# First projections in two-term pieces, setup loads in halves, and four more places for expert weights

## The reference

```python
def first_block(...):                       # x 512x1024, ctx 256x1024
    sh1, sc1, g1, sh2, sc2, g2 = adaln_params(c, w_mod)      # silu(c) @ w_mod + b_mod, six parts of 1024
    hx = modulate(rms_norm(x, norm1_g), sh1, sc1)            # h * (1 + scale) + shift
    hc = modulate(rms_norm(ctx, norm1_g), csh1, csc1)
    y_x = token_mix(hx, hc, w_in, ...)      # projections; gated scan in two directions, 4 heads;
                                            # attention, 8 heads over 2 KV heads, keys of ctx and x; gated merge
    x = x + g1 * y_x
    x = x + g2 * expert_choice_moe(modulate(rms_norm(x, norm2_g), sh2, sc2), w_router, w_gate, w_up, w_down)
    return rms_norm(x, final_norm_g)
def expert_choice_moe(h, ...):              # 16 experts, each takes its best 64 of 512 tokens
    gate, idx = top_k(softmax(h @ w_router).T, 64)
    hid = silu(h[idx] @ w_gate) * (h[idx] @ w_up)            # 1024 -> 1024, per expert
    return zeros.at[idx].add((hid @ w_down) * gate)
# second_block: projections, sparse attention, short convolution, and a feed-forward of 4096 features
```

## Time and profile before

| | us |
|---|---|
| median of 3 runs (1909.41 to 1919.11) | 1913.41 |
| the profiled execution's own time | 1913.68 |
| its span, first to last instruction | 1912.4 |
| PE busy | 1721.0 (90%) |
| DVE busy | 796.1 (42%) |
| ACT busy | 570.9 (30%) |
| mean granted TensorE clock | 0.965 of 2.4 GHz |
| bytes moved | 329.4 MB, mean 172 GB/s |

### The profile page before, as it was taken

One profiled execution on the slowest core, in us unless ns is written; L12 is line 12 of the kernel. 1 busy time (PEld: TensorE's weight loads), 2 busy tenths in 40 slices (PEclk: granted clock), 3 DMA queues, 4 the chain that ended last, 5 costly groups with the idle time before them and its releaser, 6 DMA issues.

```text
span 1912.4 us, 20334 instructions
## 1 busy us (share of the span) xinstructions
PE 1721.0 (90%) x8150; PEld 1123.7 (59%) x8150; DVE 796.1 (42%) x1325; ACT 570.9 (30%) x1026; POOL 117.2 (6%) x123
## 2 busy tenths in 40 slices
PE   5989899886999996998888888999888899999999
PEld 2656667564877773333332333687544678888877
DVE  2164655456633432021120211547577434444444
ACT  2224563564343321110110100431544442222221
POOL 0002121012100001000000000000100001010010
PEclk9999899988999997999999999999999899999999
DMA  8221201123323267999999999443400122222301
GB/s 311 89 74 44 89 23 45 67 89 132 102 75 133 95 267 277 424 424 424 422 424 424 425 423 419 152 131 88 132 1 1 45 88 88 88 88 93 111 18 45
DMA packets 93185, 329.40 MB, mean 172 GB/s; under 512 B 7828, under 2 KB 22820, under 8 KB 68516
## 3 DMA queue, kind: packets, MB, share of 16 engines
q1 hardware_dynamic: 86032, 315.80, 42.6%
q10 hardware_dynamic: 5716, 8.05, 1.3%
q0 software_dynamic: 1344, 4.25, 0.6%
HBM read 322.83 MB, written 4.20 MB: 171 GB/s over the span
## 4 chain that ended last, share of the span: by engine, by line
PE 66%; DMA 16%; DVE 9%; ACT 6%; issue 2%; ACTq 0%; SPq 0%; DVEq 0%
PE PS L672 21%; PE PS L1061 9%; PE PS L815 8%; DMA room<-in_w_exp_up_dram 8%; PE PS L413 7%; DMA ring<-in_w_exp_gate_dram 6%; PE PS L409 3%; PE PS L544 3%; PE PS L626 3%; PE PS L888 2%; PE PS L469 1%; DMA ring<-in_w_in_dram 1%; PE PS L698 1%; PE PS L826 1%; PE PS L1003 1%
## 5 line engine op out<-in xcount | busy, mean ns | idle before, releaser
L1791 DVE TENSOR_TENSOR wR<-ring,wR 128x1024 fp32r<-128x1024 f32 (+2 forms) x134 | 151.4, 1130 | 223.3 <-ACT wR L1176 223.2
L1176 ACT CAST wR<-ring 128x1024 fp32r<-128x1024 f32 (+2 forms) x134 | 130.0, 971 | 203.5 <-PE PS L1061 126.5
L1061 PE MATMUL PS<-wR,hR 128*128 128x512 f32 x768 | 176.2, 390 | 8.9 <-DVE tmp L2571 6.9
L672 PE MATMUL PS<-xR,wR 128*128 128x512 f32 x768 | 175.6, 389 | 0.9 <-DVE wR L1791 0.9
L1061 PEld LDWEIGHTS PS<-wR,hR 128*128 128x128 f32 x768 | 143.5, 188 | 41.5 <-DVE tmp L2571 9.6
L672 PEld LDWEIGHTS PS<-xR,wR 128*128 128x128 f32 x768 | 144.0, 188 | 31.1 <-issue 1.3
L815 PE MATMUL PS<-room,xeT 128*64 128x512 f32 x512 | 115.7, 595 | 27.2 <-DMA room<-in_w_exp_up_dram 15.1
L672 PE MATMUL PS<-hR,wR 128*128 128x512 f32 x528 | 128.5, 405 | 8.2 <-DVE wR L1791 5.6
L815 PE MATMUL PS<-ring,xeT 128*64 128x512 f32 x512 | 117.4, 604 | 19.3 <-DMA ring<-in_w_exp_up_dram 15.8
L672 PEld LDWEIGHTS PS<-hR,wR 128*128 128x128 f32 x528 | 103.2, 197 | 34.3 <-issue 8.7
L672 PE MATMUL PS<-hR1h,wR 128*128 128x512 f32 x320 | 102.2, 394 | 2.4 <-DVE wR L1791 2.4
(11 more groups left out here) (469 smaller groups left out, 2628.7 us busy)
## 6 DMA issues: line engine op xcount, KB each, us to landing
ring<-in_w_exp_gate_dram SPq DMA_DIRECT2D x32, 1024.0 KB, 27.6
room<-in_w_exp_gate_dram SPq DMA_DIRECT2D x32, 1024.0 KB, 28.1
ring<-in_w_exp_up_dram SPq DMA_DIRECT2D x32, 1024.0 KB, 26.4
room<-in_w_exp_up_dram SPq DMA_DIRECT2D x32, 1024.0 KB, 27.4
ring<-in_w_exp_down_dram SPq DMA_DIRECT2D x32, 1024.0 KB, 26.5
room<-in_w_exp_down_dram SPq DMA_DIRECT2D x32, 1024.0 KB, 27.8
ring<-in_w_mod_dram SPq DMA_DIRECT2D x12, 2048.0 KB, 7.9
ring<-in_w_in_dram SPq DMA_DIRECT2D x11, 2048.0 KB, 9.3
```

Of the source, the lines that this page charges most:

```text
L672: mm = T.matmul(b, o[s][:, k, :], x(t, k), start=(k == ks[0] and j == 0), stop=(k == ks[-1] and j == 2))
L1061: mm = T.matmul(down[m], uR[:, r % 2, s, k, 128 * i:128 * i + 128], o[t][:, 0, 512 * q:512 * q + 512], start=(k + j == 0), stop=(k == 3 an ...
L1176: A.copy(parts(wR, chunks, n)[0], W.view(unit)[:, ks, cs]).then_inc(act_hi.sem, act_hi.up(key))
L1791: V.tensor_tensor(lo, W.view(unit)[:, ks, cs], hi.bitcast(F32), ALU.subtract) \
```

## The change

- The first projections (`aq`, `akv`, and `f`, `q`, `v` of heads 0 and 1) become three-term products. Their weights are cut into twelve chunks (`first_chunks`), each rounded and subtracted into one of a few buffers `wS`; the tokens are stored in two pieces too (`hS`).
- The loads of the setup change order and size: `mod 0`, `mod 2` (shift and scale of features 0 to 511), the first half of `aq` (its first four k), then `mod 1`, `mod 3`, the context, the second half of `aq`. PE, ACT and DVE follow that order: `aq` runs k pair by k pair over four open banks.
- A unit of 256 columns takes one slot instead of two; slots are released by `sub_lo` instead of by PE.
- Ten small loads move from ACT's queue to POOL's, behind DVE's `low(7)`.
- `head_norm` of the queries comes before that of the keys.
- Router: logarithm and exponential instead of root and reciprocal, with the table loaded ahead; the first search round reads PSUM; the store of `h2k` in four parts; products wait for two k of `xeT` at a time.
- Experts: a ninth permanent extra place (`strips`) and three that are used once; the pieces 18, 7 and 15 are requested last of the first twenty, 18 only when `h2k` has been stored.

```diff
+MOD_ORDER = (0, 2, 1, 3)
...
+    FIRST = (0, 6, 2, 0, 4, 3)
+    ONCE = {7: "gathered", 15: "gathered", 19: "mixed"}
...
+            if k == 2 and n in self.ONCE:
+                slots = [NS + len(more) + list(self.ONCE).index(n)]
+                n += 1
+            elif k == 2:
+                if not cycle:
+                    cycle = [(at + j) % NS for j in range(NS)]
+                    cycle[4:4] = range(NS, NS + 4)
+                    cycle += range(NS + 4, NS + len(more))
+                slots = [cycle[turn % len(cycle)]]
+                turn, n = turn + 1, n + 1
             else:
-                size, top = 1 if k * n <= 2048 and k <= 4 else 2, 4 if 4 <= i < whole else NS
-                at = 0 if at + size > top or i == whole else at
+                if cycle:
+                    at, cycle = (at + turn % (NS + len(more))) % NS, []
+                size, top = 1 if k * width <= 2048 else 2, 4 if i < whole else NS
+                at = self.FIRST[i] if i < 6 else 0 if at + size > top or i in (6, whole) else at
...
+    def order(self):
+        first = self.number["gate", 0, 0, 0]
+        late = (18, 7, 15)
+        ahead = [n for n in range(20) if n not in late]
+        return [*range(first), *(first + n for n in (*ahead, *late)), *range(first + 20, len(self.units))]
...
-    u = [(("mod", j), *cols(d["w_mod"], 512 * j, 512)) for j in range(4)]
-    u += [("aq", *cols(d["w_in"], 2560, 512)), ("akv", *cols(d["w_in"], 3072, 256))]
+    first = [(("mod", j), *cols(d["w_mod"], 512 * j, 512)) for j in range(4)]
+    aq = [(("aq", x), *cols(d["w_in"][512 * x:512 * x + 512], 2560, 512)) for x in range(2)]
+    u = [first[0], first[2], aq[0], first[1], first[3], aq[1]]
+    u.append(("akv", *cols(d["w_in"], 3072, 256)))
...
+    once = [Area(nc, at, at + 2048).take(name, [128, 2048]) for name, at in
+            (("once7", DYN + 15456), ("once15", DYN + 13408), ("once19", DYN + 3072))]
...
+    first_chunks = [(("aq", k), ("aq", k // 4), slice(k % 4, k % 4 + 2), slice(0, 512), k % 4 == 2) for k in range(0, 8, 2)]
+    first_chunks += [(("akv", c), "akv", slice(4 * c, 4 * c + 4), slice(0, 256), c == 1) for c in range(2)]
+    first_chunks += [((x + "0", h), (x, 0), slice(0, 8), slice(128 * h, 128 * h + 128), h == 1) for x in "fq" for h in range(2)]
+    first_chunks += [(("v0", c), ("v", 0), slice(4 * c, 4 * c + 4), slice(0, 256), c == 1) for c in range(2)]
...
+        if chunks is first_chunks:
+            return [t.rearrange("p (a b) -> p a b", b=b) for t in ((wS1a, wS[3]) if n == 1 else wS[2 * (n % 2):2 * (n % 2) + 2])]
...
+            for k in range(4):
+                turn_x(early, k)
+            mod_turn(mods, 0)
+            mod_product(mods, 2)
+            turn_x(early, 4)
...
+        def token_terms(b, w, i, ks, start, stop):
+            for n, k in enumerate(ks):
+                for j, (s, t) in enumerate(TERMS):
+                    mm = T.matmul(b, hS(s, k, 128 * i, 128 * i + 128), w[t][:, n, :], start=(start and n + j == 0),
+                                  stop=(stop and n == len(ks) - 1 and j == 2))
+            return mm
...
+            def chunk(n, tiles):
+                w = parts(wS, first_chunks, n)
+                for i in tiles:
+                    if i == 0:
+                        T.wait_ge(*dve_lo["aq", 2 * n])
+                        for k in range(2 * n, 2 * n + 2):
+                            T.wait_ge(*dve_in["lx", k])
+                    if n == 0:
+                        bs.append(four.take(T, ("aq", i), act_in["aq", i]))
+                    mm = token_terms(bs[i], w, i + 2, range(2 * n, 2 * n + 2), n == 0, n == 3)
...
+            chunk(0, range(4))
+            mod_product(mods, 1)
+            mod_product(mods, 3)
+            chunk(1, range(2))
+            mod_turn(mods, 1)
+            mod_turn(mods, 3)
+            chunk(1, range(2, 4))
...
+            chunk(2, range(4))
...
+            chunk(3, range(4))
+            pool = Banks(0, 8)
+            bs = []
+            for c in range(2):
+                T.wait_ge(*dve_lo["akv", c])
+                w = parts(wS, first_chunks, 4 + c)
+                if c == 0:
+                    T.wait_ge(*dve_in["lc", 7])
+                for i in range(6):
+                    if c == 0:
+                        bs.append(pool.take(T, ("akv", i), act_in["av", i]))
+                    mm = token_terms(bs[i][:, 0:256], w, i, range(4 * c, 4 * c + 4), c == 0, c == 1)
...
+            for h in range(2):
+                b = pool.take(T, ("f", 0, h), act_scan["f", 0, h], 2)
+                T.wait_ge(*dve_lo["f0", h])
+                w = parts(wS, first_chunks, 6 + h)
+                feature_terms(b[:, 0:512], w, 256, 768)
+                feature_terms(b[:, 512:768], w, 0, 256).then_inc(pe_scan.sem, pe_scan.up(("f", 0, h)))
...
+        W.free["gathered"] = s_ga, 16
         router()
+        W.free["strips"] = pe_moe["aff"]
...
+            squares(range(2, 6), s_x)
+            root(2, 6)
+            A.wait_ge(*dve_in["A1", 0])
+            tokens(1)
+            copy_hi(wS, first_chunks, 0)
+            tokens(3)
+            copy_hi(wS, first_chunks, 1)
+            squares(range(2), s_x2)
+            copy_hi(wS, first_chunks, 2)
+            A.wait_ge(*dve_in["A1", 1])
+            tokens(5)
+            tokens(7)
+            root(0, 2)
+            copy_hi(wS, first_chunks, 3)
             for k in range(8):
                 A.wait_ge(*pe_in["hc", k | 1])
-                o = 256 * (k % 2)
-                A.activation(hT[:, k, 0:256], bank(("hc", k & 6))[:, o:o + 256], ACT.Identity, bias=modc[:, k, 1:2],
-                             scale=A1[:, 1, k:k + 1]).then_inc(s.sem, s.up(("hc", k)))
+                b = bank(("hc", k & 6))[:, 256 * (k % 2):256 * (k % 2) + 256]
+                for to, key in ((hT[:, k, 0:256], "hc"), (hSc[:, k, :], "hic")):
+                    A.activation(to, b, ACT.Identity, bias=modc[:, k, 1:2], scale=A1[:, 1, k:k + 1]) \
+                        .then_inc(s.sem, s.up((key, k)))
...
+            copy_hi(wS, first_chunks, 4)
             for i in range(4):
                 A.wait_ge(*pe_in["aq", i])
                 A.copy(aq[:, i, :], bank(("aq", i))).then_inc(s.sem, s.up(("aq", i)))
+            copy_hi(wS, first_chunks, 5)
+            root("q", 32)
+            copy_hi(wS, first_chunks, 6)
             for i in range(6):
                 A.wait_ge(*pe_in["akv", i])
                 A.copy(akv[:, i, :], bank(("akv", i))[:, 0:128]).then_inc(s.sem, s.up(("ak", i)))
                 A.copy(avs[:, i, :], bank(("akv", i))[:, 128:256]).then_inc(s.sem, s.up(("av", i)))
-            A.wait_ge(*dve_in["lb"])
-            A.activation(lbt[:, 1:3, :], lbt[:, 1:3, :], ACT.Exp).then_inc(s.sem, s.up("lb"))
-            for name in ("k", "q"):
-                A.wait_ge(*dve_in["ms", name])
-                n = {"k": 12, "q": 32}[name]
-                A.activation(rr[:, 0:n], rr[:, 0:n], ACT.Sqrt).then_inc(s.sem, s.up(("rms", name)))
+            copy_hi(wS, first_chunks, 7)
+            root("k", 12)
...
+            A.activation(spare, eps, ACT.Ln).then_inc(s.sem, s.up())
             for g in (pe_mix.end, pe_mm[("wo", 7), 0], dve_mix.end, dve_lo[("wo", 7)], act_mix.end):
                 A.wait_ge(*g)
             A.wait_ge(*pe_moe["square"])
-            A.activation(rinvc, bank("square")[:, 0:32].rearrange("p (i x) -> p i x", x=8)[:, :, 0], ACT.Sqrt, bias=eps,
-                         scale=1.0 / (32 * 1024)).then_inc(s.sem, s.up("rms"))
+            inverse_root(rinvc, bank("square")[:, 0:32].rearrange("p (i x) -> p i x", x=8)[:, :, 0], 1.0 / (32 * 1024), s, "rms")
...
+                A.dma_start(h2d[128 * i:128 * i + 128, :], h2k[:, i, :]).then_inc(s_h2, 16)
...
+            norm(2, 6)
+            scale(2, 6)
+            for j in (0, 2):
+                mod_rows(j)
+                mod_cols(j)
+            gains(0)
+            tokens(0)
+            tokens(2)
+            low(0)
+            low(1)
+            sub_lo(wS, first_chunks, 0)
+            low(2)
+            low(3)
+            sub_lo(wS, first_chunks, 1)
+            for j in (1, 3):
+                mod_rows(j)
+            for j in (1, 3):
+                mod_cols(j)
+            gains(1)
+            tokens(4)
+            tokens(6)
+            low(4)
+            low(5)
+            sub_lo(wS, first_chunks, 2)
+            norm(0, 2)
+            low(6)
+            low(7)
+            scale(0, 2)
+            sub_lo(wS, first_chunks, 3)
+            for k in range(8):
+                V.wait_ge(*act_in["hic", k])
+                V.tensor_tensor(hS(1, k, 0, 256), hT[:, k, 0:256], hS(0, k, 0, 256).bitcast(F32), ALU.subtract) \
+                    .then_inc(s.sem, s.up(("lc", k)))
...
+            V.wait_ge(*act_in["aq", 3])
+            sub_lo(wS, first_chunks, 5)
+            head_norm(s, q4, 4, 8, gb[:, 0, :], 0.125, tA, rr, ("ms", "q"), act_in["rms", "q"])
+            sub_lo(wS, first_chunks, 6)
```

(22 more changed lines are left out.)

326 lines of the change are left out of this document (188 added, 138 removed).

## The result

The changed kernel takes 1893.5 us (median of 4 runs, 1888.7 to 1897.0) against 1914.1 before (4 runs, 1909.4 to 1919.1): ratio 0.989, 95% interval 0.9856 to 0.9924. The profiled execution spans 1893.1 us, 19.3 less than before. The prediction of 1892 (1881 to 1906, faster) held.

What follows compares the result with a forecast made beforehand. Almost wholly PE work bounds the chain before the experts, weight loads by DMA the expert stage. The first stage's 10.8 plus 10.5 from router and places gave 21.3 us off 1913.7: 1892, range 1881 to 1906.

Steps and rivals of the forecast that it cites:

- Part 1: First projections: three-term instead of true fp32 products save 18.8 us of PE, 5.5 in aq and 13.3 behind it.
- Part 2: Setup loads in halves: chunk 0 at about 36 at the lower clock, akv at 76, 6 to 8 us later than before.
- Part 3: From akv to the weave: 13.3 and 6.2 us off, 1.5 added for pauses; weave at 148, 10.8 earlier.
- From the weave to the router nothing changes. Cost nothing, gain nothing.: Weave to router: PE work unchanged, loads never waited for; no gain and no cost.
- Part 4: Router: Ln and Exp gain nothing, with a table load between; dropped copy and earlier first expert product give 1.1 us.
- Part 5: Experts: four more pieces loaded ahead in the DMA pause save 9.9 us, less 0.5 for a delayed first gather.
- its bound of 5: First gather: piece 18 and the split stores may delay it by at most 5 us, with 0.5 taken.
- upper bound of 13: Router and expert places together: gain 10.5 us, with bounds 6 and 13.
- B: First stage gives nothing, as pauses before chunks 0, 2 and akv lower the clock and sub_lo is late; 1903 us, chance 0.19.
- C: First stage gives nearly all its PE saving and more, 17 to 20 us, chunk 0 starting warm; 1884 us, chance 0.20.
- D: Expert places buy nothing: added pieces hold up the gather, or a later pause uses up the gain; 1902 us, chance 0.07.
- E: Slower than before: masks late on POOL's queue delay sub_lo 5 and everything behind; 1933 at 5 us per issue, chance 0.04.

Runs made afterwards that it cites:

- experiment 2: Changed kernel with plain true fp32 products of unrounded operands in aq, akv, f0, q0 and v0 instead of three terms; 1912.7 us, ratio 0.9994.
- experiments 7: Changed kernel with 38 unused identity transposes on PE filling the pause before chunk 0 alone; 1894.2 us.
- experiment 8: Changed kernel with unused identity transposes in four first-stage PE pauses: before the turns of x, chunk 0, chunk 2 and akv; 1887.0 us, ratio 0.9869.
- 3: Changed kernel with both halves of aq's weights requested behind mod 0, mod 2, mod 1 and mod 3; 1893.6 us, ratio 0.9896.
- experiment 9: Changed kernel with 138 unused identity transposes in six PE pauses of the weave; 1893.2 us, ratio 0.9909.
- experiment 1: Changed kernel with the old 16 places for expert pieces and the old request order; 1904.7 us, ratio 0.9958.
- experiment 4: Changed kernel with the router's square root and reciprocal back, root and exponential tables both loaded ahead by spare activations; 1894.2 us.
- 5: Changed kernel with the strips' piece requested after the first gather has landed instead of right ahead of the gather; 1892.6 us, ratio 0.9904.
- experiment 12: Changed kernel with the ten small loads issued from ACT's queue again, behind the context evictions, instead of POOL's; 1902.6 us, ratio 0.9945.

## Why the prediction was right, and where not

- **Part 1 (18.8 us of PE, 13.3 behind the start of akv).** The size was about right: experiment 2 has 12.2 behind the start of `akv`, and 1.8 of aq's part, which I had put at nothing, in front of it.
- **Part 2 (chunk 0 at 36 at the lower level, chunk 2 at 58.5 to 60, akv at 76).** Right, each within 0.2 us. The mechanism (PE's own pace and the pauses) is shown by experiments 7 and 8; that the halves bring little, by 3. The clock was at the lower level only for the first 14 of chunk 0's products.
- **Part 3 (weave at 148, 10.8 earlier).** 148.8, 10.0 earlier; the wait for q0's load is gone, and experiment 2 puts what that and the release bring at 5.0, where I had 6.2 less 1.5 for pauses. The masks' landing was sized wrong (6 us after the issue, measured 10.2), at no cost by luck of 0.6 us.
- **"From the weave to the router nothing changes. Cost nothing, gain nothing."** This failed: +3.9 us. I had put this stretch at nothing because its work is the same, without pricing the clock behind its pauses. At one place (137.9 against 141.2) the clock fell behind a pause behind which it had not fallen before, and this makes 3.3 of the 3.9; experiment 9 gets those 3.3 back there. The other 0.6 are open.
- **Part 4 (1.1 us, a load between Ln and Exp).** Right: 1.05 in experiment 1, and the load is there at 705.73. By "ScalarE: Activation LUTs", section "Table sets: the hidden batching unit", of the Trainium skill there would be no load between them, and the trace does not agree; experiment 4 shows what its rule could have given in front of the index, 1.25 us, and that the gather would have kept only 0.1 of it.
- **Part 5 (9.9 us of pieces, 0.5 for the gather).** The pieces: 10.8 by the distance, 9.8 to 11.8 by experiment 1. The term that was mis-sized is the gather's, 0.5 put in and 1.4 to 1.7 measured (1, 5), inside its bound of 5. The upper bound of 13 comes from no term that is named: 9.9 and 1.1 give 11. The last `up` product came at 1155.4 and not at 1150, through this and the weave.
- **Behind the last up product** I had put nothing; it was -2.9. The lost clock is 1.7 less (22.2 to 20.5); the rest is open, and two executions of the changed kernel differ by as much (698.8 and 696.1). It made up for most of the weave's loss, so that 19.3 in place of 21.3 looks closer than the steps were: that is luck.
- **The rivals.** B falls (the first stage gave 10.0); C falls, though experiment 8 shows that its 17 to 20 us were there to be had once the pauses are filled (18.6); D falls with experiment 1. E's masks were nearer than I said, but experiment 12 shows that a landing 3 us too late costs nothing to be seen.

## What to carry to other kernels

Before crediting a shorter engine stage, walk the small steps in front of each chunk: here the new order, copies and subtractions put the second projection 9 us later, and only the cheaper products and the load wait that went turned that into a gain. Where an engine idles a few us in front of a long stage, price the clock behind the pause as well, and if pauses are filled, fill all on the chain: the first alone brought at most 0.4 us here, four brought 8.6. When a wait is removed on the way to a transfer, look at once for the next one it needs (here the stores, which were hidden by only 0.4 us), and count what shares the DMA with it.
